# Attention's value products moved behind the next round's scores, and the gate items' matmuls taken token block by token block

## The reference

```
h = RMSNorm(x)
z = h @ W_in + b_in              # 8448 columns: q/k/v of attention A, u/v of B, q/k/v of C, three gates
A: sliding-window (128) attention, 16 query heads on 4 key/value heads, a learned sink per head
B: u * (tril(W_s) LayerNorm(v) + b) in chunks of 128 tokens
C: dilated window attention, 3 groups of 4 heads, group outputs weighted by softmax denominators
merged = sum_i sigmoid(gate_i) * (branch_i @ P_i);  x = x + merged @ W_out
x = x + HierMoE(RMSNorm(x))      # 32 experts, one group of 8 per token, the top 2 inside it
```

## Time and profile before

| | |
|---|---|
| median of three executions | 1019.53 us |
| the profiled execution | 1016.57 us |
| its span | 1014.8 us |
| TensorE busy with matmuls | 955.4 us (94%) |
| TensorE busy with weight loads | 668.1 us (66%) |
| VectorE busy | 560.6 us (55%) |
| ScalarE busy | 431.0 us (42%) |
| GpSimd busy | 58.1 us (6%) |
| mean rate of the DMAs | 308 GB/s |

### The profile page before, as it was taken

How to read it: one execution, slowest core, us unless ns; L and a number is a source line. 1 busy time by engine, 2 the same in 40 slices (tenths; PEclk the granted TensorE clock), 3 DMA queues, 4 the chain that set the end, 5 groups by cost and what they waited for, 6 DMA issues and landing times.

```text
span 1014.8 us, 15601 instructions
## 1 busy us (share of the span) xinstructions
PE 955.4 (94%) x5898; PEld 668.1 (66%) x5898; DVE 560.6 (55%) x1328; ACT 431.0 (42%) x920; POOL 58.1 (6%) x74
## 2 busy tenths in 40 slices
PE   9999999999999995986999999999999999987787
PEld 7888877778886441632588888777888954444333
DVE  8666787786883332120276668788868634122212
ACT  5434666766444120211354355666764441111122
POOL 1120400000010000000004004000000100000000
PEclk9999999999999999898999999999999999989989
DMA  9975543249999999999997755332599999999996
GB/s 346 355 251 185 199 132 126 84 123 323 362 386 422 411 426 423 426 428 427 418 395 246 238 181 193 125 125 73 175 351 344 410 421 407 425 425 426 426 426 279
DMA packets 99162, 313.03 MB, mean 308 GB/s; under 512 B 13424, under 2 KB 22672, under 8 KB 76560
## 3 DMA queue, kind: packets, MB, share of 16 engines
q1 hardware_dynamic: 98752, 312.04, 80.3%
q10 hardware_dynamic: 336, 0.02, 0.0%
HBM read 310.20 MB, written 1.84 MB: 308 GB/s over the span
## 4 chain that ended last, share of the span: by engine, by line
PE 80%; DMA 10%; SPq 4%; DVE 2%; issue 1%; ACT 1%; DVEq 0%; POOLq 0%; POOL 0%
PE ps L1496 16%; PE ps L1497 15%; PE ps L1498 15%; PE ps L2167 7%; DMA arena<-in_w_expert_up_dram 5%; DMA ring_rest<-in_w_expert_down_dram 5%; SPq L513 4%; PE ps L2141 4%; PE ps L2253 3%; PE ps L2241 3%; PE ps L1619 2%; PE ps L1521 2%; PE ps L1631 2%; PE ps L2110 2%; PE ps L1647 1%
## 5 line engine op out<-in xcount | busy, mean ns | idle before, releaser
L1148 DVE TENSOR_TENSOR split_w<-arena,split_w 128x512 fp32r<-128x512 f32 (+1 forms) x352 | 233.0, 700 | 100.6 <-ACT split_w L941 97.0
L1496 PE MATMUL ps<-split_w,split_a 128*128 128x512 f32 (+1 forms) x736 | 283.8, 386 | 0.1
L1498 PE MATMUL ps<-split_w,split_a 128*128 128x512 f32 (+1 forms) x736 | 277.0, 376 | 0.0
L1497 PE MATMUL ps<-split_w,split_a 128*128 128x512 f32 (+1 forms) x736 | 276.7, 376 | 0.0
L941 ACT CAST split_w<-arena 128x1024 fp32r<-128x1024 f32 (+1 forms) x171 | 175.9, 1031 | 177.1 <-PE ps L1498 170.5
L1496 PEld LDWEIGHTS ps<-split_w,split_a 128*128 128x128 f32 x736 | 138.5, 188 | 26.8 <-issue 2.2
L1498 PEld LDWEIGHTS ps<-split_w,split_a 128*128 128x128 f32 x736 | 138.4, 188 | 25.8
L1497 PEld LDWEIGHTS ps<-split_w,split_a 128*128 128x128 f32 x736 | 138.7, 189 | 23.2
L2398 DVE SCALAR_TENSOR_TENSOR acts<-ps,wslot,acts 128x256 f32<-128x256 f32 x16 | 7.7, 484 | 166.2 <-ACT acts L2063 144.1
L2167 PE MATMUL ps<-arena,rows 128*32 128x512 f32 x416 | 90.5, 617 | 5.1 <-DMA arena<-in_w_expert_up_dram 5.1
L2167 PE MATMUL ps<-ring_rest,rows 128*32 128x512 f32 x352 | 76.4, 637 | 12.5 <-DMA arena<-in_w_expert_up_dram 12.5
(11 more groups left out here) (284 smaller groups left out, 1067.5 us busy)
## 6 DMA issues: line engine op xcount, KB each, us to landing
arena<-in_w_in_dram SPq DMA_DIRECT2D x62, 1024.0 KB, 5.3
arena<-in_w_expert_down_dram SPq DMA_DIRECT2D x36, 1024.0 KB, 18.6
arena<-in_w_expert_gate_dram SPq DMA_DIRECT2D x34, 1024.0 KB, 24.0
arena<-in_w_expert_up_dram SPq DMA_DIRECT2D x32, 1024.0 KB, 24.0
ring_rest<-in_w_expert_down_dram SPq DMA_DIRECT2D x24, 1024.0 KB, 17.5
ring_rest<-in_w_expert_gate_dram SPq DMA_DIRECT2D x22, 1024.0 KB, 23.6
ring_rest<-in_w_expert_up_dram SPq DMA_DIRECT2D x22, 1024.0 KB, 25.5
arena<-in_w_proj_a_dram SPq DMA_DIRECT2D x8, 1024.0 KB, 5.0
```

Source lines behind the costliest of these rows:

```text
L1148: dve.tensor_tensor(wlo[:, jj % 2, cols], half_slot(jj, w)[:, cols], whi[:, jj % 2, cols].bitcast(F32), ALU.subtract).then_inc(low_split i ...
L1496: pe.matmul(o, hi, rhs_hi, start=first, stop=False)
L1497: pe.matmul(o, hi, rhs_lo, start=False, stop=False)
L1498: return pe.matmul(o, lo, rhs_hi, start=False, stop=last)
```

## The change

On TensorE the products of batch b are no longer the last thing in `pv(b)`: they are a function of their own, called in round b+1 behind the scores of batch b+2 and ahead of the turning of batch b+1's probabilities. On ScalarE the copy of their result moves along, ahead of the copies of the turned probabilities. In a gate item the order is now token block 1 with both k blocks, then token block 0 with both; the two waits for the low halves stand in token block 1, ahead of the first and of the fourth matmul, `z_half` is raised by the sixth matmul, and the work `between` still lies behind six matmuls.

```
@@ ScalarE, the rounds
+                            if b >= 1:
+                                o_out(b - 1)
                             pv_out(b)
                             if b == 8:
                                 qk_out(b + 2, 0, 1)
...
                             if b + 1 < BATCHES:
                                 exps(b + 1)
-                            if b < BATCHES - 1:
-                                o_out(b)
@@ TensorE, gate items (z_conv loses its arguments between, order and free)
                         def gates_conv(j, between=None):
 
-                            z_conv(j, 6, TAIL if j >= 4 * CHUNKS else BANK, j + 1, between, (1, 0),
-                                   2 * (j // 4) if j > 4 * AHEAD else None)
+                            w = TAIL if j >= 4 * CHUNKS else BANK
+                            for tb in (1, 0):
+                                if between and tb == 0:
+                                    between()
+                                for kk in range(2):
+                                    if tb:
+                                        pe.wait_ge(low_split if kk else low_first, j + 1)
+                                    kb = 2 * (j % 4) + kk
+                                    if kb == 0 and j > 4 * AHEAD:
+                                        pe.wait_ge(z_evac, 2 * (j // 4) - tb)
+                                    mm = three_passes(ps[:, 6 + tb, 0:w], kb, tb, whi[:, j % 2, kk * w:(kk + 1) * w],
+                                                      wlo[:, j % 2, kk * w:(kk + 1) * w], kb == 0, kb == KB - 1)
+                                if tb and j % 4 == 3:
+                                    mm.then_inc(z_half, 1)
+                            mm.then_inc(conv_used, 1)
@@ TensorE, the rounds
                             gates_conv(45 + 2 * b, (lambda: turn_probs(b, 2)) if b >= 8 else None)
+
+                        def products_of(b):
                             if b < 8:
                                 product_pair(b)
                             elif b % 2:
...
                                 scores(b + 1)
+                                products_of(b - 1)
                                 pv(b)
```

More of the change, by code:

```diff
@@ L1498, in three_passes, with z_conv @@
                             return pe.matmul(o, lo, rhs_hi, start=False, stop=last)
-                        def z_conv(jj, bank, w, ready, between=None, order=(0, 1), free=None):
+                        def z_conv(jj, bank, w, ready):
                             for kk in range(2):
-                                if kk and between:
-                                    between()
                                 pe.wait_ge(low_split if kk else low_first, ready)
                                 kb = 2 * (jj % 4) + kk
-                                for tb in order:
-                                    if free is not None and kb == 0:
-                                        pe.wait_ge(z_evac, free - tb)
+                                for tb in range(TB):
                                     mm = three_passes(ps[:, bank + tb, 0:w], kb, tb, whi[:, jj % 2, kk * w:(kk + 1) * w],
                                                       wlo[:, jj % 2, kk * w:(kk + 1) * w], kb == 0, kb == KB - 1)
-                                    if order[0] and tb and kb == KB - 1:
-                                        mm.then_inc(z_half, 1)
                             mm.then_inc(conv_used, 1)
```

## The result

The changed kernel took 1026.22 us (median of four executions, 1023.95 to 1027.95), the kernel before 1019.38 us beside it: a ratio of 1.0070, 95% interval 1.0055 to 1.0086. It is 6.8 us slower; 6.2 had been forecast. The profiled execution of the changed kernel took 1023.95 us against 1016.57 before.

The account below looks back on a forecast made before the run. TensorE was taken to bound the attention rounds. Waits of 3 x 0.76 + 0.99 + 1.1 less savings of 1.0 and 0.25 lose 3.1 us a layer, 6.2 for two: 1025.7 us from 1019.53, eight-in-ten range 1022.4 to 1029.5.

Parts of the forecast that it names:

- The bound and its passage: Attention rounds: TensorE busy 94.74 of 95 us, so a change there passes one for one to the end.
- The savings: Rounds 0 to 6: each moved block of products saves 0.14 us, 1.0 a layer; round 7 saves 0.25.
- The one unknown: Entering products from scores was taken to cost no more than entering the turning; 1.6 us either way over two layers.
- The wait in rounds 1, 3, 5: The fourth weight load of the next gate item waits for VectorE's second low half, costing 0.76 us per round.
- The returned 0.13: After a waiting weight load the next matmul starts 0.34 us later instead of 0.47, giving back 0.13.
- Rounds 7 and 9: Items 60 and 64 wait for the low half: 0.99 us lost in round 7 before 0.25 saved, 1.1 in round 9.
- Its copy was called covered: ScalarE's 0.4 us copy of the products' result, moved ahead of the turned copies, was to delay nothing.
- Only the savings count: Rival: TensorE never waits for the second low halves, 2.9 us gained, 1016.6 us; chance 0.07.
- The two cancel: Rival: waits stand but each move saves 0.3 us; 1022.8, or 1021 with a third of the waits covered; chance 0.07.
- No wait spread to the turning: Rival: lateness spreads through ScalarE's copies and exponentials, so the turning waits in odd rounds too; 1034 us, chance 0.08.
- the granted clock stayed 1.00: Rival: the clock falls in TensorE's new gaps, 3.5 us per 7 us stretch at half clock; 1029 to 1033, chance 0.03.
- the earlier eviction of block 1 is of no use: Odd rounds: block 0's eviction still waits for the chunk's last matmul, and the second low half stands behind it.

Follow-up runs that it names:

- low_mid: Changed kernel, but in odd rounds VectorE makes the second low half between the evictions of block 1 and block 0; 1017.44 us against 1019.30 before.
- low_mid_keep9: Changed kernel with the second low half between the two evictions and the 24 products left in round 9; 1017.25 us against 1018.64 before.
- copy_behind: Changed kernel, but ScalarE copies the products' result behind the copies of the turned probabilities; 1023.87 us against 1019.30 before.
- order_only: Kernel before with only the gate items' token order changed, products and ScalarE's copy in their old place; 1019.63 us against 1019.30 before.

## Why the prediction was right

*The bound and its passage.* TensorE bounds the rounds, and what is lost in them reaches the end one for one: 3.5 us in layer 0 are 3.8 behind its experts, and the two layers' losses are 7.2 us at the end of the trace. The measured 6.8 at the medians agrees. That small gains pass through as fully isn't shown: in the profiled execution of low_mid the 0.4 us gained before layer 0's experts are 2.1 us lost behind them, which is of the size by which the executions of one kernel scatter, and low_mid_keep9 shows only about half of its gain at the end.

*The savings.* 0.14 per moved block was forecast, 0.13 to 0.15 per even round measured. The one unknown, entering the products from the scores, cost what I took: the step from the last score to the first product is 0.31 us, as that to the turning was. The Trainium skill (TensorE: Matmul & The Clock Gate, Part 2, Step-by-step) has a weight load pulled ahead of running matmuls where the row groups don't conflict or the background buffer is its target. The trace shows no such pull at this switch: the products' loads again start with the products, after 0.33 us.

*The wait in rounds 1, 3, 5.* Forecast 0.76, measured 0.79 to 0.81 (item 48 takes 3.73 us to the scores where an item after two transposes takes 2.93). The returned 0.13 after a waiting load was there: 0.35 us from that load to the next matmul.

*Rounds 7 and 9.* Round 7 was forecast at 0.74 net and measured at 0.83; round 9 was forecast at 1.1 and measured at 1.06. The wait of round 9's first matmul was not forecast, and it is hidden behind the one that was. In layer 0 alone another 0.09 us lies in the turning of the third head in item 65 (0.38 us; in layer 1 it is 0.29, as before the change), and its cause is open. Together 3.44 and 3.32 instead of 3.1 a layer, 6.8 instead of 6.2.

*ScalarE.* Its copy was called covered. copy_behind agrees: the rounds don't change by more than the layers differ.

*The rivals.* "Only the savings count" needed the low half 0.9 us behind the last matmul's start instead of 1.77; it came at 1.78 (149.15 against 147.37). low_mid brought it to 0.39 (147.76), and the savings then did count. "The two cancel" needed 0.3 us saved per move, and 0.13 to 0.15 was measured. No wait spread to the turning (0.7 us as before), and the granted clock stayed 1.00 in the rounds.

What I had not seen is that the change was one line away from a gain. The prediction says that the earlier eviction of block 1 is of no use, since block 0's is what the low half stands behind. It stops there and doesn't ask what else VectorE could do in the 0.63 us that this opens.

## What to carry to other kernels

When independent work is moved away from between two dependent pieces, list what it was covering, by name and with its time of readiness against the new time of need; here it covered an eviction and an operand split on another engine. An accumulation order that completes one bank early is worth something only if the reader's engine has its list arranged to use the gap. And when a change that removes real cost comes out slower, look for the in-order list whose head now waits while its next entry could run.

## What the runs showed of the hardware

When a weight load had to wait for a semaphore, the matmul behind its own started 0.34 to 0.35 us after the load (149.20 to 149.55, 203.22 to 203.56 in the changed kernel). In a running stream it was 0.47 us, so 0.13 us of each wait came back. The switch between full-array matmuls and half-array tiles cost 0.09 to 0.10 us on the way in (0.32 us from a projection matmul to the first score or product, where it is 0.23 to a transpose) and on the way out (0.20 us from the last product to a transpose, 0.10 to a further pair of products). It cost as much between the two kinds of tile: 0.31 us from a pair of scores to a product, as to a transpose before the change, where it is 0.21 from such a pair to the next score. Putting the two kinds of tile next to each other saved one switch per block. The order of the twelve matmuls of an item, bank by bank or alternating, cost TensorE nothing (rounds 0 to 6 of order_only keep their length to 0.00 us).

The rounds of one kernel repeat to 0.1 us between two layers and, where nothing is changed, to 0.01 us between kernels, while the end times of one kernel scatter by 2 to 5 us. Outside the rounds, matched matmul by matmul, the traces of two kernels move against each other mostly between 400 and 520 us and behind 890 us, where the experts' weights fill the DMA queues.
